# Giving one of three score banks to the transposed probabilities in a two-layer decoder trunk

## What is computed

```python
def nsa(q, k_slc, v_slc, k_win, v_win, kc, vc, gates):    # per tile of 128 queries, per group of 4 heads
    pc    = masked_softmax(q @ kc.T, mc)                   # 32 compressed keys
    o_cmp = pc @ vc
    o_slc = masked_softmax(q @ k_slc.T, causal) @ v_slc    # all 8 blocks are chosen at 512 tokens
    o_win = masked_softmax(q @ k_win.T, causal) @ v_win    # window of 512
    return gates[0] * o_cmp + gates[1] * o_slc + gates[2] * o_win
# then: mix = concat(y_ret, y_nsa) @ w_out, norm, x +=, conv-MLP, norm, x +=
```

## The kernel before

| job | at item | bank before, waits for exps of | bank after, waits for exps of |
| --- | --- | --- | --- |
| 18, 19 | 7 | 1, job 15; 2, job 16 | 1, job 16; 2, job 17 |
| 20 | 8 | 3, job 17 | 1, job 18 |
| 21 | 10 | 1, job 18 | 2, job 19 |
| 22, 23 | 12, 13 | 2, job 19; 3, job 20 | 1, job 20; 2, job 21 |
| 24 | 14 | 1, job 21 | 1, job 22 |
| 25 to 28 | 15, 17, 18, 19 | each the third before it | each the second before it |
| 29, 30, 31 | 20, 21, 22 | each the third before it | each the second before it |
| 32, 33 | 24, 25 | 3, job 29; 1, job 30 | 1, job 30; 2, job 31 |
| 34 | 26 | 2, job 31 | 1, job 32 |
| 35, 36, 37 | 27, 28, 31 | each the third before it | each the second before it |
| 38 to 43 | 32 to 42 | 1 and 2 in turn, job 43 in 1 | unchanged, bank and wait |

## Time and profile before

### The profile page before, as it was taken

The page is one execution under the profiler, slowest core; times in us unless marked ns, Lnnn a source line. Parts: engine busy times, 40 slices in busy tenths (PEclk is TensorE's granted clock), DMA queues, the critical chain, the costliest instruction groups (busy, mean ns, idle before and its releaser), DMA issues.

```text
span 1367.5 us, 17661 instructions
## 1 busy us (share of the span) xinstructions
PE 1345.5 (98%) x6888; PEld 1112.7 (81%) x6888; DVE 724.8 (53%) x910; ACT 599.9 (44%) x1037; POOL 699.0 (51%) x544
## 2 busy tenths in 40 slices
PE   8999999999999999999999999999999999999998
PEld 5889877778888888888888888777798888888886
DVE  5406659745545445644462075687455545456444
ACT  5223568745433333432451335686463333334221
POOL 2644678753544444544465446786544444445441
PEclk9999999999999999999999999999999999999999
DMA  5433330031333223323233334100333233333331
GB/s 207 137 102 105 112 93 16 1 124 64 122 93 106 94 93 98 102 93 93 63 123 104 115 98 139 34 14 6 119 110 105 94 93 101 100 93 93 102 98 61
DMA packets 34882, 127.18 MB, mean 93 GB/s; under 512 B 3952, under 2 KB 4464, under 8 KB 34416
## 3 DMA queue, kind: packets, MB, share of 16 engines
q1 hardware_dynamic: 34656, 125.53, 29.3%
q10 hardware_dynamic: 144, 0.52, 0.1%
HBM read 123.94 MB, written 2.10 MB: 92 GB/s over the span
## 4 chain that ended last, share of the span: by engine, by line
PE 88%; DVE 5%; ACT 3%; issue 1%; POOL 1%; DMA 1%; DVEq 0%; POOLq 0%; ACTq 0%; SPq 0%
PE bank L1769 34%; PE bank L1801 18%; PE bank L1419 17%; PE bank L1435 5%; PE bank L1663 3%; PE bank L1701 2%; PE bank L1609 1%; DVE s_bias L1217 1%; PE bank L1523 1%; PE bank L1630 1%; PE bank L1610 1%; PE bank L1728 1%; PE bank L1727 1%; DVE pt_l L952 1%; PE bank L1387 1%
## 5 line engine op out<-in xcount | busy, mean ns | idle before, releaser
L554 POOL TENSOR_TENSOR w_lo<-raw,w_hi 128x1024 fp32r<-128x1024 f32 x216 | 520.9, 2418 | 474.5 <-ACT w_hi L655 474.2
L655 ACT ACTIVATE w_hi<-raw 128x1024 fp32r<-128x1024 f32 x220 | 231.0, 1055 | 242.1 <-DMA raw<-wstream 242.0
L1769 PE MATMUL bank<-act_hi,w_hi 128*128 128x512 f32 (+1 forms) x768 | 286.1, 373 | 0.8 <-DVE act_lo L952 0.6
L1769 PE MATMUL bank<-act_hi,w_lo 128*128 128x512 f32 (+1 forms) x768 | 285.4, 372 | 0.0
L1769 PE MATMUL bank<-act_lo,w_hi 128*128 128x512 f32 (+1 forms) x768 | 285.3, 372 | 0.0
L911 ACT ACTIVATE cv<-bank,par 128x512 f32<-128x512 f32 x88 | 68.4, 778 | 286.0 <-PE bank L1769 286.0
L1348 DVE SCALAR_TENSOR_TENSOR cv<-bank,par,cv 128x511 f32<-128x511 f32 x88 | 66.0, 750 | 225.2 <-ACT cv L911 225.2
L1769 PEld LDWEIGHTS bank<-act_hi,w_hi 128*128 128x128 f32 x768 | 144.7, 188 | 27.0 <-DVE act_lo L952 1.6
L1769 PEld LDWEIGHTS bank<-act_lo,w_hi 128*128 128x128 f32 x768 | 144.7, 188 | 25.0
L1769 PEld LDWEIGHTS bank<-act_hi,w_lo 128*128 128x128 f32 x768 | 144.7, 188 | 24.9
L1419 PE MATMUL bank<-w_hi,act_hi 128*128 128x512 f32 (+1 forms) x384 | 144.6, 376 | 0.6 <-DVE w_lo L952 0.5
(11 more groups left out here) (177 smaller groups left out, 2168.2 us busy)
## 6 DMA issues: line engine op xcount, KB each, us to landing
raw<-wstream SPq DMA_DIRECT2D x220, 512.0 KB, 3.6
g_all<-gains SPq DMA_DIRECT2D x2, 2048.0 KB, 7.4
x_out<-x SPq DMA_DIRECT2D x8, 256.0 KB, 2.0
x<-x_in SPq DMA_DIRECT2D x3, 512.0 KB, 9.2
const<-consts SPq DMA_DIRECT2D x1, 1030.0 KB, 13.8
g_all<-gains ACTq DMA_DIRECT2D x1, 512.0 KB, 5.1
x<-x_in SPq DMA_DIRECT2D x2, 256.0 KB, 5.1
par<-pars SPq DMA_DIRECT2D x2, 235.0 KB, 3.5
```

The costliest lines, as they stand in the source:

```text
L554: nc.gpsimd.tensor_tensor(w_lo[:, s, :], raw_slot(s), r32(w_hi[:, s, :]), ALU.subtract)\
L655: nc.scalar.activation(w_hi[:, s, :], raw_slot(s), ACT.Copy).then_inc(hi_ready, 1)
L1769: last = mm(bank[:, b, first:end], a, v, start=(k == 0 and n == 0), stop=(k == KD - 1 and n == 2), skip_group_check=True)
```

## The change

`S_BANK` goes round three banks for jobs 0 to 14 only, and round banks 1 and 2 from job 15 on (before: from job 38). `PT_BANK` goes round banks 4, 5 and 3 for items 6 to 23, and round 4 and 5 for all others. `turn_p(k)` now waits for the remainder of the last item in the same bank: three items back inside items 6 to 23 (two before). The first item in bank 3, item 8, waits for the exponentials of job 14. The output projection of token tile 3, which takes bank 3 from item 30 on, waits for item 23's remainder too. No instruction is added, removed or moved on any engine, and no buffer in SBUF changes; only which bank is addressed and which count is waited for.

```diff
-        S_BANK = lambda z: 1 + z % 3 if z < 38 else 1 + z % 2 if z < 42 else 1
+        S_BANK = lambda z: 1 + z % 3 if z < 15 else 1 + z % 2 if z < 42 else 1
         LAST_IN_BANK = lambda z: max(y for y in range(z) if S_BANK(y) == S_BANK(z))
-        PT_BANK = lambda k: 4 + k % 2
+        TRIPLE = range(6, 24)
+        PT_BANK = lambda k: (4, 5, 3)[k % 3] if k in TRIPLE else 4 + k % 2
...
                             z = max(z for z in range(len(JOBS)) if S_BANK(z) == t)
                             pe.wait_ge(e_done, upto(e_done, l, heads_through[z]))
+                            if t == 3:
+                                pe.wait_ge(ptl, upto(ptl, l, TRIPLE[-1] + 1))
...
                 def turn_p(k):
                     n, v, j = ITEMS[k]
-                    if k >= 2:
-                        pe.wait_ge(ptl, upto(ptl, l, k - 1))
+                    same = [m for m in range(k) if PT_BANK(m) == PT_BANK(k)]
+                    if same:
+                        pe.wait_ge(ptl, upto(ptl, l, same[-1] + 1))
+                    elif PT_BANK(k) == 3:
+                        z = max(z for z in range(len(JOBS)) if S_BANK(z) == 3)
+                        pe.wait_ge(e_done, upto(e_done, l, heads_through[z]))
                     else:
                         pe.wait_ge(q_l, upto(q_l, l, 4))
                         pe.wait_ge(vc_f, upto(vc_f, l, 1))
```

## The result

The change makes the kernel slower: 1377.35 us median of 6 executions (1374.98 to 1380.03), against 1370.18 for the kernel before; the ratio is 1.0048, 95% interval 1.0035 to 1.0061, or +6.6 us (4.8 to 8.4). The two medians themselves differ by 7.2. The executions spread over 5 us, and the six of the kernel before over 6.7 (1369.49 to 1376.19). The medians alone are therefore too coarse to settle effects of a microsecond or two.

The account below looks back on a forecast made before the run. PE, busy 98% of the span, was taken as the bound. Waits less absorbed stalls gave 3.2 us a layer, +6.4 us in two, 1375.7 us on the profiled execution and 1376.8 us median; 8-in-10 range 1374.2 to 1379.4 us.

Parts of the forecast that it names:

- What bounds: Whole kernel: PE's own work, busy 98% of the span, plus its idle time; the change acts only through idle time.
- The waits at jobs 20, 24 and 34: Scores waiting for exponentials two jobs back: job 20 +2.62 us, job 24 shift to +1.50, job 34 +1.80, per layer.
- Job 29's own wait: Item 20, waiting for job 27's exponentials: adds 0.19 us, lifting PE's shift to 1.35 us.
- What the old stalls absorb: Stalls at transposes of items 10 (0.87 us), 13 and 14 (0.84), 17 (0.34) take in new lateness each layer.
- Job 36 and the projection: After job 34 in each layer: job 36 waits for job 34's exponentials, 0.05 us added, shift 3.2 us.
- The gain side: Transposes of items 10, 13, 14 and 17 lose their stalls: at most 2.05 us a layer, at least nothing.
- "faster" rival: Jobs 20 and 34 would not wait, leaving only the gain: up to 4.1 us, 1366.3 us; chance 0.03.
- The sum: 3.2 us a layer, +6.4 us over two layers, 1375.7 us on the profiled execution, median 1376.8 us.
- The clock rival: Stall of 2.6 us halves clock from job 20 to 34: at most 33 us a layer, 1436 us; chance 0.01.
- signs of being wrong: Job 20 waiting under 2 us, item 24 later by under 0.8 or over 2.5 us, granted clock leaving 1.00.

Follow-up runs that it names:

- wait20: The kernel before with one wait changed, job 20 waiting for job 18's exponentials instead of job 17's; median 1374.89 us, ratio 1.0038.
- wait34: The kernel before with one wait changed, job 34 waiting for job 32's exponentials instead of job 31's; median 1371.89 us, ratio 1.0015.
- job34_b3: The changed kernel with job 34 in bank 3, waiting for item 23's transposes there and not for job 32; median 1377.54 us, ratio 1.0046 to the kernel before.
- scores_two: The kernel before with only the scores' half of the change: two score banks from job 15, transposes on two banks; median 1379.60 us, ratio 1.0067.
- y_moved_third: The kernel before with retention-output transposes moved, freeing bank 0 as third bank for transposed probabilities in items 6 to 13; median 1380.66 us, ratio 1.0066.
- second set: The changed kernel run once more without edit; median 1379.20 us of 6 executions, ratio 1.0065 to the kernel before.
- wait20_filled: The kernel before with job 20 waiting for job 18's exponentials and ten unread matmuls ahead of that wait; median 1372.01 us, ratio 1.0013.
- before_again: The kernel before run once more without edit, for the clock; median 1370.76 us, ratio 1.0002.

## Why the prediction was right, and where it was off

*What bounds.* Right. The same PE work, and only PE's idle time moved, until the clock came in.

*The waits at jobs 20, 24 and 34.* Right in place, order and size. Job 20: forecast 2.62, measured 2.60, in both layers (896.82 against 891.58 less the 2.64 at item 2 of that layer). Job 34: its wait moved PE from 1.24 (job 29 at 240.20, against 237.29) to 3.03, 1.79 against 1.80. Job 29's own wait added 0.12 where 0.19 was reckoned. Job 24 waits because DVE was late by 1.03, as reckoned. Jobs 20 and 34 were tested by themselves (wait20, wait34 and job34_b3). Job 24 was not, but in scores_two it starts 229.82 - 227.56 less the 0.73 at item 2, 1.53 late, with PE waiting 0.30 there instead of 0.68: its place is set by what it waits for and not by when PE arrives.

*What the old stalls absorb.* The step rested on a late PE finding the remainders ready. scores_two and wait20 show it: on two banks item 10's stall is gone all the same. The term was mis-sized between items 10 and 14: 1.40 us absorbed where 0.84 was reckoned (+0.33 measured, +0.91 forecast). The stalls of items 11 and 12, too short for a bracket, were left out (they took in 0.44 us together), and four transposes that do not wait take 0.60 us instead of 0.66. Part of it came back at once: the product right behind the transposes of item 14 starts at 229.30 and is 229.30 - 227.01 - 1.67 = 0.62 late, because it needs the remainder that DVE finishes at 228.57 + 0.68 = 229.25. None of this mattered in the end, since job 24's wait set the shift anew.

*Job 36 and the projection.* I added 0.05 for job 36, which did not wait, and overlooked that the projection at item 26 already began 0.18 late in the kernel before (249.63, for a reason that no row lists), which job 34's delay swallowed. So a layer loses 2.85 us and not 3.2.

*The gain side.* I took 2.05 us a layer for an upper bound and said that the products wait for the same remainder. That is nearly all of it: y_moved_third shows the waits going from the transposes to the products, with 0.4 us a layer left, and scores_two shows 0.3. The "faster" rival was never near, and its price was too high even with free banks.

*The sum.* The waits give 5.7 us (1372.9 and 1373.2 against 1367.3 at equal clock) where I said 6.4. The rest of the measured 6.6, and of the 8.9 of the second set, is clock.

*The clock rival.* Here the prediction was wrong in the chance, 0.01, and in the price, 66 us. The last of the signs of being wrong that it names, that the granted clock leaves 1.00, came true. The mechanism exists. It struck in eight of ten profiled layers, lasted 3.4 to 10.2 us and not 33, and cost at most half its length. From the mean clocks it takes 0.9 us (first set, against 0.9962) to 3.4 us (second). That the forecast median of 1376.8 lies so close to 1377.35 owes something to two errors of opposite sign, 0.7 us too much for the waits and nothing for the clock. That closeness is partly luck. The reason that I gave against the clock rival, no such stretch after stalls of 0.87 us, was a reading about short stalls and said nothing of one three times as long. The Trainium skill, TensorE: Matmul & The Clock Gate, section on PSUM-queue depth-cycling, says that short idle moments of TensorE between groups of matmuls, with PSUM banks taken in turn, make the clock swing between its levels; wait20 and wait20_filled bear out the direction. The cost here is the runs' alone.

Left open: why job 34's 1.63 us has no such effect while the waits of 1.7 us at line 1520 (1519 before) have it in 13 of 26 (before_again, too, is at half clock behind them, at 164 and 840 us), and why two of ten layers with 2.4 us escape; what PE did in the microseconds around may matter, and no run here separated it from the length.

## What to carry to other kernels

When a buffer is moved from one ring to another, follow for each ring the wait that is behind the one you remove: here the product needed the same remainder as the transposes, so the extra bank only moved the stall by one instruction, while the ring that gave the bank had a round trip (scores, minima, exponentials) longer than two jobs at three places. Reckon each moved wait from the end of the work it now waits for, and carry the shift of every engine along, since a stall that an engine would have had anyway absorbs a new one. A wait of a couple of microseconds on TensorE can cost nearly as much again in clock (wait20: 3.1 us at equal clock and 2.4 us by its lower mean clock). If the wait cannot be avoided, put work there, even useless work. And try first to place the work elsewhere before changing how many buffers it has.

## What the runs showed of the hardware that I had not expected

- Behind 2.4 us of idle PE the granted clock went to half for 3.4 to 10.2 us in eight of ten profiled layers, and filling the idle time with ten unread matmuls kept it at 1.00.
- The mean clock differs between executions of one kernel (0.993 to 1.000 for the kernel before) and explains most of the spread of the times (four fifths of the variance within a kernel, over all kernels): 0.99 us per 0.001. For effects under 0.5% it is worth comparing at equal clock.
- The same small DVE instruction, the last of the gate's in layer 1, takes 0.16 us in nine of the 13 profiles and 2.2 to 2.3 us in four, whatever the kernel; no run shows why. In the profile of the kernel before it was slow and on PE's path, in that of the changed one it was not, which gave back about 1.6 us there:

```profile
792.72 2.31 DVE L1056 TENSOR_SCALAR gate<-gate 128x24 f32<-128x24 f32 x1
```
```profile
796.34 0.16 DVE L1057 TENSOR_SCALAR gate<-gate 128x24 f32<-128x24 f32 x1
```
